# Linear attention: the product of the decayed q and the state in three f16 passes in place of one f32 matmul

## The reference, cut to what matters

```python
def _gla_chunk_step(S, inp):
    qc, kc, vc, gc = inp
    bc = jnp.cumsum(gc, axis=1)
    o_inter = jnp.einsum('bthd,bhde->bthe', qc * jnp.exp(bc), S)
    ...
    o_intra = jnp.einsum('bhts,bshe->bthe', att, vc)
    b_last = bc[:, -1]
    S_new = jnp.exp(b_last)[..., None] * S + jnp.einsum(
        'bshd,bshe->bhde', kc * jnp.exp(b_last[:, None] - bc), vc)
    return S_new, o_inter + o_intra
```

## Time and profile before

| | |
|---|---|
| runs | 2242.24 us median of 3 (2241.82 to 2243.98) |
| the profiled execution | 2240.97 us, of it a span of 2239.3 us |
| GLA recurrence in that span | from about 816 to 1412 us |
| TensorE busy over the span | 97% |

### The profile page before, as it was taken

The page is one execution under the profiler, slowest core; times in us unless marked ns, Lnnn a source line. Parts: engine busy times, 40 slices in busy tenths (PEclk is TensorE's granted clock), DMA queues, the critical chain, the costliest instruction groups (busy, mean ns, idle before and its releaser), DMA issues. The chain is left out here.

```text
span 2239.3 us, 34220 instructions
## 1 busy us (share of the span) xinstructions
PE 2168.3 (97%) x12858; PEld 1089.7 (49%) x12858; DVE 1384.6 (62%) x2174; ACT 1137.8 (51%) x2165; POOL 1046.5 (47%) x790
## 2 busy tenths in 40 slices
PE   8999999999899899999999999899899999999998
PEld 4555555554344444444445444344465554444443
DVE  6999999987654534544534544577558885445232
ACT  7766665577774333543434434433358885334111
POOL 2988888878888222112122121276248887000000
PEclk9999999999999999999999999999999999999999
DMA  6011011024335142210301112355536664103222
GB/s 220 29 48 44 29 45 44 29 101 135 105 119 182 43 61 67 63 41 19 84 20 30 21 35 66 113 159 144 157 71 118 124 101 81 62 1 104 95 94 94
DMA packets 237723, 178.99 MB, mean 80 GB/s; under 512 B 188847, under 2 KB 208943, under 8 KB 236536
## 3 DMA queue, kind: packets, MB, share of 16 engines
q1 hardware_dynamic: 237560, 176.81, 29.3%
HBM read 96.65 MB, written 35.80 MB: 59 GB/s over the span
## 5 line engine op out<-in xcount | busy, mean ns | idle before, releaser
L1179 DVE SCALAR_TENSOR_TENSOR cv_tap_sum<-cv_glu,cv_prm,cv_tap_sum 128x1024 f32<-128x1024 f32 x326 | 418.9, 1288 | 11.9 <-ACT cv_tap_sum L667 2.4
L932 POOL TENSOR_TENSOR mixed<-mixed,cv_tap_products 128x1024 f32<-128x1024 f32 x153 | 364.0, 2379 | 77.6 <-ACT cv_tap_products L682 62.2
L101 PE MATMUL cv_proj<-H_hi,cv_w_ga 128*128 128x416 f16 (+1 forms) x640 | 216.8, 339 | 8.0 <-DVE H_lo L1152 8.0
L102 PE MATMUL cv_proj<-H_lo,cv_w_ga 128*128 128x416 f16 (+1 forms) x640 | 216.8, 339 | 0.0
L103 PE MATMUL cv_proj<-H_hi,cv_w_ga 128*128 128x416 f16 (+1 forms) x640 | 216.7, 339 | 0.0
L101 PE MATMUL gm_vr<-gm_wvr_hi,H_hi 128*128 128x512 f16 x512 | 195.3, 381 | 0.0
L102 PE MATMUL gm_vr<-gm_wvr_lo,H_hi 128*128 128x512 f16 x512 | 194.5, 380 | 0.0
L103 PE MATMUL gm_vr<-gm_wvr_hi,H_lo 128*128 128x512 f16 x512 | 194.2, 379 | 0.0
L1987 POOL TENSOR_TENSOR gm_q_inter<-gm_q_rel,gm_block_decays 128x512 f32<-128x512 f32 x16 | 16.8, 1048 | 373.2 <-ACT gm_block_decays L2077 373.2
L682 ACT ACTIVATE cv_tap_products<-cv_glu,cv_prm 128x1024 f32<-128x1024 f32 x138 | 151.6, 1138 | 35.9 <-POOL mixed L932 35.8
L2091 ACT ACTIVATE gm_v_r<-gm_vr 128x256 f16<-128x256 f32 x68 | 26.1, 384 | 276.5 <-PE gm_vr L103 272.6
(11 more groups left out here) (470 smaller groups left out, 5539.2 us busy)
## 6 DMA issues: line engine op xcount, KB each, us to landing
cv_w_stage<-conv_w SPq DMA_DIRECT2D x24, 512.0 KB, 4.0
mixed<-gla_w SPq DMA_DIRECT2D x8, 1024.0 KB, 5.3
go_rows<-h_rows SPq DMA_DIRECT2D x16, 512.0 KB, 4.2
h_rows<-go_rows SPq DMA_DIRECT2D x16, 512.0 KB, 3.2
pl_sums_a<-h_rows SPq DMA_DIRECT2D x16, 512.0 KB, 3.5
out<-pl_sums_a SPq DMA_DIRECT2D x16, 512.0 KB, 2.6
cv_tap_products<-gate_z SPq DMA_DIRECT2D x24, 256.0 KB, 4.6
mixed<-xT SPq DMA_DIRECT2D x12, 416.0 KB, 8.5
```

Source lines behind the costliest of these rows:

```text
L101: nc.tensor.matmul(out, w_hi, x_hi, start=first, stop=False)
L102: nc.tensor.matmul(out, w_hi, x_lo, start=False, stop=False)
L932: nc.gpsimd.tensor_tensor(c_unit(U), c_unit(U), prod[:, r % 3, :], ALU.add).then_inc(s_add, 1)
L1179: nc.vector.scalar_tensor_tensor(out=acc_unit(U), in0=window(U, k), scalar=col(U // 2, k), in1=acc_unit(U), op0=ALU.mult, op1=ALU.add).the ...
```

## The change

The decayed q is kept as two f16 halves in place of one f32 tile. GpSimd makes them with three operations a group in place of one: the f32 product, for which it borrows the tile `k_state`, the same product again rounded to f16, and their difference. The state gets two f16 halves as well. ScalarE copies S to its high half (`state_high`) right after `high`, and VectorE subtracts it from S (`state_low`) right after `low`, both in the slot after the update of S. TensorE waits for `s_Sl` (the low half of the state) where it waited for `s_S`, and issues three f16 passes.

```diff
--- before.py
+++ after.py
@@ -1697,7 +1697,8 @@
         smd = m.sb("block_logs", [P, NSM])
         sme = m.sb("block_decays", [P, 3, NSM])
         q1, k1 = m.sb("q_rel", [P, 2, GROUP]), m.sb("k_rel", [P, 2, GROUP])
-        qi, kd = m.sb("q_inter", [P, 2, GROUP]), m.sb("k_state", [P, GROUP])
+        qh = [m.sb("q_inter_hi", [P, 2, GROUP], F16), m.sb("q_inter_lo", [P, 2, GROUP], F16)]
+        kd = m.sb("k_state", [P, GROUP])
         kh = [m.sb("k_state_hi", [P, GROUP], F16), m.sb("k_state_lo", [P, GROUP], F16)]
         kdT = [m.sb("k_rows_hi", [P, 2, 4, P], F16), m.sb("k_rows_lo", [P, 2, 4, P], F16)]
         firstT = [m.sb("first_k_rows_hi", [P, 1, P], F16), m.sb("first_k_rows_lo", [P, 1, P], F16)]
@@ -1707,6 +1708,7 @@
         kv = [None] + [m.sb(f"k_block{I}", [P, 2, 4, (I + 1) * BLK]) for I in (1, 2, 3)]
         vr = m.sb("v_r", [P, VSLOTS, 2 * DV])
         S = m.sb("state", [P, DV])
+        Sh = [m.sb("state_hi", [P, DV], F16), m.sb("state_lo", [P, DV], F16)]
         att32 = m.sb("att_masked", [P, P])
         att = [m.sb("attT_hi", [P, P], F16), m.sb("attT_lo", [P, P], F16)]
         og = m.sb("gated", [P, 3, DV])
@@ -1741,6 +1743,7 @@
         s_se, s_eq, s_ek = m.sem("block_decays"), m.sem("exp_q"), m.sem("exp_k")
         s_q1, s_k1 = m.sem("q_rel"), m.sem("k_rel")
         s_kv = m.sem("group_ready")
+        s_q32, s_qh, s_Sh, s_Sl = m.sem("q_inter"), m.sem("q_inter_hi_done"), m.sem("state_hi_done"), m.sem("state_lo_done")
         s_kd, s_kh, s_kl, s_kt = m.sem("k_state"), m.sem("k_state_hi_done"), m.sem("k_state_lo_done"), m.sem("k_rows_turned")
 
         s_vr, s_v, s_re, s_rl, s_rg, s_rs = (m.sem("vr_psum"), m.sem("v_done"), m.sem("r_exp"), m.sem("r_log"),
@@ -1984,8 +1987,16 @@
                         pool.wait_ge(s_q1, Q(hd, G))
                         if free is not None:
                             pool.wait_ge(s_o, ROWS(free))
-                        nc.gpsimd.tensor_tensor(blocks(buf(qi, 2, G, w)), blocks(buf(q1, 0, G, w)), spread(e[:, OM:OM + nb], bl),
-                                                ALU.mult).then_inc(s_kv, 1)
+                        if g:
+                            pool.wait_ge(s_kl, g)
+                        src, dec = blocks(buf(q1, 0, G, w)), spread(e[:, OM:OM + nb], bl)
+                        q32, hi, lo = blocks(kd[:, :]), blocks(qh[0][:, G % 2]), blocks(qh[1][:, G % 2])
+                        nc.gpsimd.tensor_tensor(q32, src, dec, ALU.mult).then_inc(s_q32, 1)
+                        nc.gpsimd.tensor_tensor(hi, src, dec, ALU.mult).then_inc(s_qh, 1)
+                        pool.wait_ge(s_q32, Q(hd, G))
+                        pool.wait_ge(s_qh, Q(hd, G))
+                        nc.gpsimd.tensor_tensor(lo, q32, hi, ALU.subtract).then_inc(s_kv, 1)
+                        pool.wait_ge(s_kv, KV(hd, G) - 3)
                     pool.wait_ge(s_k1, g + 1)
                     if g:
                         pool.wait_ge(s_kl, g)
@@ -2103,6 +2114,15 @@
                     b = (row - 1) % 3
                     nc.scalar.activation(turn_rows[:, 0, b, :], og[:, b], ACT.Copy).then_inc(s_hi, 1)
 
+                def state_high(hd, c):
+                    cc = hd * NCH + c
+                    act.wait_ge(s_S, cc + 1)
+                    if (v := past(ROW(hd, c))) is not None:
+                        act.wait_ge(s_o, v)
+                    if cc:
+                        act.wait_ge(s_Sl, cc)
+                    nc.scalar.activation(Sh[0][:, :], S[:, :], ACT.Copy).then_inc(s_Sh, 1)
+
                 def squares(hd, G, c, off, n):
                     row = ROW(hd, c)
                     act.wait_ge(s_o, row)
@@ -2121,6 +2141,7 @@
                         hd, G, c, off, n = CHUNKS[i - LEAD - 1]
                         if c:
                             high(hd, c)
+                        state_high(hd, c)
                     if V:
                         evac(V[0], V[2], V[4])
                     if R:
@@ -2235,12 +2256,13 @@
                     v_ = [v_half(h, cc, r) for h in range(2)]
                     pe.wait_ge(s_vl, cc + 1)
                     if c:
-                        pe.wait_ge(s_S, cc)
+                        pe.wait_ge(s_Sl, cc)
                         if (v := past(ROW(hd, c) - 1)) is not None:
                             pe.wait_ge(s_og, v)
                             pe.wait_ge(s_sq, v)
                         pe.wait_ge(s_atl, ROW(hd, c))
-                        nc.tensor.matmul(p_o[0:n, 0:DV], buf(qi, 2, G, w)[:, off:off + n], S[:, :], start=True, stop=False)
+                        q_ = [x[:, G % 2, off:off + n] for x in qh]
+                        three_pass(nc, p_o[0:n, 0:DV], *q_, Sh[0][:, :], Sh[1][:, :], True, False)
                         three_pass(nc, p_o[:, 0:DV], att[0][0:n, :], att[1][0:n, :], *v_, False, True).then_inc(s_o, 1)
                     pe.wait_ge(s_kt, k_turned(group_of(hd, G)))
                     if (v := past(cc)) is not None:
@@ -2343,6 +2365,11 @@
                     room_turned(dve, row)
                     b = (row - 1) % 3
                     nc.vector.tensor_tensor(turn_rows[:, 1, b, :], og[:, b], turn_rows[:, 0, b, :], ALU.subtract).then_inc(s_lo, 1)
+                def state_low(hd, c):
+                    cc = hd * NCH + c
+                    dve.wait_ge(s_Sh, cc + 1)
+                    nc.vector.tensor_tensor(Sh[1][:, :], S[:, :], Sh[0][:, :], ALU.subtract).then_inc(s_Sl, 1)
+
                 def rows(hd, G, c, off, n):
                     cc, bl = hd * NCH + c, min(n, BLK)
                     if c:
@@ -2376,6 +2403,8 @@
                     dve.wait_ge(s_ds, cc + 1)
                     if (v := past(ROW(hd, c))) is not None:
                         dve.wait_ge(s_o, v)
+                    if cc:
+                        dve.wait_ge(s_Sl, cc)
                     if c == 0:
                         nc.vector.tensor_copy(S[:, :], p_s[:, 0:DV]).then_inc(s_S, 1)
                         return
@@ -2401,6 +2430,7 @@
                             hd, G, c, off, n = CHUNKS[i - LEAD - 1]
                             if c:
                                 low(hd, c)
+                            state_low(hd, c)
                     if V:
                         v_lo(V[0], V[2], V[4])
                     if V and V[2]:
```

## The result

Over nine runs each, the changed kernel takes 2247.79 us (2246.08 to 2249.34), the kernel before 2242.80 (2241.82 to 2243.98): ratio 1.0023, interval 1.0013 to 1.0033. That is **5.0 us slower**: a small difference, but the interval does not reach 1, so it is a real one. The median lies 0.2 us beyond the upper end of the range predicted (2238.6 to 2247.6). The profiled execution took 2247.13 us with a span of 2245.4.

A forecast was written before the change was run, and what follows sets the result against it. TensorE's own issue was taken to bound the recurrence. The terms, -5.5 + 3.0 + 2.7 + 0.3 = +0.5 us, gave 2242.7 us against the runs, no difference (chance 0.62), with 2238.6 to 2247.6 for 8 in 10.

The forecast's parts named there:

- 0.107 a pass and 0.32 for three: TensorE, ordinary slots: three f16 passes take 0.32 us where the f32 matmul takes 0.43, saving 0.11 a chunk.
- Hidden, with 0.32 to spare: Ordinary slots: `state_low` is ready 0.32 us before TensorE comes to it, so the new wait costs nothing.
- 6 x 0.48 + 0.1 = 3.0 us lost: Last 7 slots: TensorE waits for `state_low` behind the scores' low half, 0.48 us net in six, about 0.1 in one.
- GpSimd's own part: GpSimd's added product and difference, 2.2 us a group, are covered by its waits and cost nothing.
- The stages behind, which I take as unchanged: After the recurrence: the later stages were assumed not to move; the forecast would be wrong if they did.
- the slots at chunk 13: Three slots where `low` and `state_low` run beside GpSimd: 0.9 us net each, 2.7 us lost (1.9 to 3.9).
- 0.3 us lost in all: Other slots beside GpSimd, chunks 1, 5, 9 and 14: `state_low` just hidden or slightly late; ends 0 and 3.1 us.
- rival 1: `state_low` collides with GpSimd, deciding at chunks 1, 5, 9: +6.5 us with longer low clock, 2248.7 us; chance 0.22.
- 51 are left: Slots where TensorE is the bound and keeps the saving: 51 x 0.107 = 5.5 us gained.
- my +0.5: Whole kernel: the sum of the forecast's gains and losses, +0.5 us, meaning no difference.
- Rival 2: The f32 matmul costs more than its 0.43 us, so 0.2 a chunk is saved: -5.1, 2237.1 us; chance 0.16.
- Rival 3: The losses don't come because `state_low` is ready before the scores' half; chance included in the 0.16 of Rival 2.

The follow-up runs named there:

- e5: The changed kernel with VectorE's subtraction for the state's low half done twice, first into a spare tile: 2252.00 us, ratio 1.0044 against the kernel before.
- e3: The kernel before, with GpSimd also making q's two halves into spare tiles that nobody reads: 2242.83 us against 2242.73.
- e8: The kernel before, with ScalarE and VectorE also making the state's two halves, which nobody reads: 2242.96 us against 2242.70.
- e4: The kernel before, with three f16 passes over a constant zero tile in place of the product with the state: 2234.45 us, ratio 0.9963.
- e1: The changed kernel with `state_low` moved between mask and turned scores and `state_high` ahead of `high`: 2235.10 us against 2242.58 for the kernel before.
- e7: The changed kernel with `state_low` between mask and turned scores and GpSimd's group-1 q operations at the group's end: 2235.03 us, 0.9967 against the kernel before.
- e2: The changed kernel with GpSimd's three group-1 q operations behind its wait for the turned k_state: 2247.48 us, 1.0020 against the kernel before.
- e6: The changed kernel with GpSimd's three group-1 q operations at the very end of the group: 2247.18 us, 1.0022 against the kernel before.
- e10: The changed kernel, with GpSimd's two differences waiting at the head changes until `state_low` is done: 2244.10 us against 2242.73 for the kernel before.
- e9: The kernel before with the state's halves made but unread, and TensorE waiting for the low half before its f32 matmul: 2250.23 us, ratio 1.0037.

## Why the prediction was wrong

**Right.** "0.107 a pass and 0.32 for three": the starts are 0.11 apart and the bound slots gain 0.10 to 0.11. "Hidden, with 0.32 to spare": no wait there, and e5 used the slack up without a loss. "6 x 0.48 + 0.1 = 3.0 us lost" in the last slots: 2.8, with a wait of 0.78 in the last but one where it was 0.15; of the last two slots one loses 0.44 and the other 0.05, though not the one that I had named. GpSimd's own part and ScalarE's `state_high` at nothing: e3 and e8 show it. "The stages behind, which I take as unchanged": they differ by 1.7 us between the two profiles, within what ten others show.

**The step that failed** is that of the slots at chunk 13: "With 0.75 twice TensorE starts ... 1.34 later ... I take 0.9 net". The place, the neighbour and the wait were right and written down; the price of the subtraction beside GpSimd was too small. I read the 0.56 and 0.75 of the earlier trace rows as what an operation costs *beside* GpSimd, and carried the larger over as an upper end. The runs show another rule. In the twelve traces, 58 times a `low` or a `state_low` (in e5 its copy as well) started while a GpSimd operation of 1 us or more still had over 0.16 us to run. All 58 ended 0.28 us after that operation (0.27 to 0.29), 35 times beside a product and 23 times beside a difference; they took 0.46 to 1.38 us, by how early in it they had started. Nor did 0.75 fall outside this: in the earlier trace rows GpSimd's product ends at 938.84 + 1.05 = 939.89, and `low` at 939.42 + 0.75 = 940.17, 0.28 later. So the row did hold the price, if it is read by the ends and not by the duration. For a `state_low` that starts just after GpSimd's difference it is 1.16 + 0.28 less the small head start.

In the slot as I had drawn it, the difference ends at about 933.5, so `state_low` ends at about 933.8 and TensorE starts at 933.95, 1.8 later than 932.15 and not 1.34. The wait grew by just that, from 0.47 to 2.29 in each of the three slots. Less the 0.04 that the three passes give back there (0.68 against 0.64), the term would have been 3 x 1.76 = 5.3. Measured: chunks 12 and 13 together +4.2 where I had +2.7; the rest of it went to chunk 14 with head 2's low clock.

**A second term**, chunk 14, "0.3 us lost in all": I had -0.3 for its saved passes and up to 0.36 a slot for the collision, and measured +1.7. The collision is 0.30 of waiting in head 0, within my ends; in heads 1 and 2 TensorE does not wait, and they lose because the low clock lasts longer (head 1) or comes later (head 2). I had the clock only in rival 1.

**A third**, "51 are left": 45 are. At chunks 10 and 11 of heads 0 to 2 TensorE starts the masked scores 0.41 after the matmul ahead where it was 0.31, and so gives back the 0.10 gained. In the timeline after, the mask stands behind the weight splitting on VectorE:

```profile
896.91 1.29 DVE L2304 SCALAR_TENSOR_TENSOR gm_wqk_lo<-mixed,gm_wqk_hi 128x512 f16<-128x512 f32 x2
...
898.12 0.28 DVE L2379 TENSOR_TENSOR gm_att_masked<-gm_att,gm_mask 128x128 f32<-128x128 f32 x1
...
898.46 0.33 PE L2250 MATMUL gm_o<-gm_ident,gm_att_masked 128*128 128x128 f32 x1
```

This chain does not start from line 2243. I used that argument for chunk 12 (where the slot did gain, and chunk 13 took it back) and not for these, because a wait of 0.1 us has no entry in the table of waits. Cost: 0.6 us.

Against my +0.5 these are +1.5, +1.7 and +0.7, with -0.2 for the last slots: +4.2, against +4.4 in the trace.

**The rivals.** What happened is rival 1 by its mechanism: 2248.7 us by its sum with the longer low clock, 2247.8 measured. That the two lie so close is in part luck. The rival priced the collision at 0.75, which is too little at chunk 13, and had 3.1 us for chunks 1, 5, 9 and 14, where 0.30 was waited; the place that I gave as deciding, chunks 1, 5 and 9, lost nothing. The rule that I set beside this term (the Trainium skill, GPSIMD Engine Reference, 1. Specifications) agrees with the runs: the collision struck VectorE's operations with two SBUF inputs, 0.41 to 1.37. Those with an input in PSUM stayed as they were: the low half of the scores took 0.29 and that of v 0.41 to 0.43 whether or not a GpSimd operation with 0.3 us or more to go was running when they started, which was so 42 and 72 times in the twelve traces. Rival 2 is excluded slot by slot by e4. Rival 3 does not occur in the change, and e1 is what it describes, made by another order. The chances fell short in one way: I took the longest duration in the rows for an upper bound, while it only showed how late in GpSimd's operation that one had started.

**What stays open.** The clock's part is seen and not controlled. The number of low stretches at the three head changes was 3 before, 4 in the change, 5 in e5, 1 in e1, e4 and e7, 3 in e2, e3, e6, e8 and e10, and 2 in e9; I can say what one costs and not when one comes. So of e1's 7.5 us about 3 may depend on that. The parts do not add up in the times: e4 (-8.1) and e9 (+7.5) give -0.6 where the change shows +5.0. The clock can account for that gap: by the mean granted clock of the runs, e4 loses 3.9 us less to it than the runs beside it and e9 as much as they, and the change's runs (0.9869) some 2 us more than the runs of the kernel before in the experiments (0.9877 to 0.9879). That leaves the two collisions, of q in the change and of k in e9, to be about equal, which no run shows by itself.

## What to carry to other kernels

When a matmul is split into halves, put the operation that makes the last half into idle time of its engine *before* the wait that already sets the pace, not behind it: here the same instructions were 5.0 us slower in one order and 7.5 us faster in the other. Before pricing a new VectorE operation with two SBUF inputs, look for what GpSimd runs at the moment it starts, whatever kind of operation that is, and let it end 0.3 us after that one, not by a duration from another row. One held operation leads to the next: what follows it on VectorE starts when GpSimd's next operation has just begun, and can be held for the whole of that. And moving the GpSimd operation is no cure where GpSimd is busy through the neighbouring slots; have it wait for a moment, or take the VectorE operation away from there.

## What the runs showed that I had not expected

- A VectorE subtraction of two SBUF tiles (128 x 256, 0.41 alone) that starts while a long GpSimd operation (1.05 to 1.35 us) has over 0.16 us to go ends 0.28 us after it, without an exception in 58 cases. It makes no difference whether that is a product or a difference, of q or of k. Started 0.06 to 0.25 into a difference it took 1.20 to 1.38, and started 0.12 to 0.28 into a product 1.20 to 1.27 in e2, e9 and e10; later starts are held for less.
- One held operation can bring on the next. In the change VectorE's next operation starts 0.20 after the end of GpSimd's product and GpSimd's next one 0.14 after it, so that `state_low` begins 0.06 too late and is held for a whole difference.
- Whoever starts first goes first. Before, at head 1, `low` began 0.17 ahead of k's difference, at 1100.03, and took 0.41, and the difference took 1.27 in place of 1.16. In e6 one took 1.35, and in e1 products took up to 1.32 in place of 1.05.
- Within the recurrence TensorE's clock at 0.50 comes at the head changes, in pieces of 3.4 us, or of 6.8 when two join. In e4 TensorE's waits are those of the kernel before, and yet the number fell from 3 to 1; small shifts at these places decide over 1.7 us each. It also falls around the end of the recurrence, where TensorE waits over 7 us for the next stage: for 10.2 us before and in the change, for 13.7 in e1, where it begins at 1400.2 and slows the last slot.
